# The first two output tiles of feed-forwards and mixers worked on together, and one residual taken a tile ahead

## What is computed

```python
def rmsnorm(x, g, eps=NORM_EPS):
    y = xf * lax.rsqrt(jnp.mean(xf * xf, axis=-1, keepdims=True) + eps)
    return y.astype(x.dtype) * g
def swiglu(h, w_gate, w_up, w_down):
    return (jax.nn.silu(h @ w_gate) * (h @ w_up)) @ w_down
for l in range(DEPTH):                                  # DEPTH = 2
    x = x + 0.5 * swiglu(rmsnorm(x, ffn1_norm[l]), ...)  # D_FF = 2752
    h = rmsnorm(x, mix_norm[l])
    p_a, p_b, p_c = _split(h @ w_in[l], (A_IN, B_IN, C_IN))
    ...                                                  # three mixers
    x = x + jnp.concatenate([o_a, o_b, o_c], axis=-1) @ w_out[l]
    x = x + 0.5 * swiglu(rmsnorm(x, ffn2_norm[l]), ...)
return rmsnorm(x, final_norm)
```

## Time and profile before

| | |
|---|---|
| Median of 3 runs | 4101.9 us (4096.93 to 4108.23) |
| The profiled execution | 4107.6 us |
| its span | 4105.8 us, mean granted TensorE clock 0.976 |
| TensorE busy | 3915.6 us, 95% |
| VectorE busy | 2526.2 us, 62% |
| ScalarE busy | 1961.6 us, 48% |
| GpSimd busy | 238.7 us, 6% |

### The profile page before, as it was taken

How to read it: one execution, slowest core, us unless ns; L and a number is a source line. 1 busy time by engine, 2 the same in 40 slices (tenths; PEclk the granted TensorE clock), 3 DMA queues, 4 the chain that set the end, 5 groups by cost and what they waited for, 6 DMA issues and landing times.

```text
span 4105.8 us, 60273 instructions
## 1 busy us (share of the span) xinstructions
PE 3915.6 (95%) x25080; PEld 3089.6 (75%) x25080; DVE 2526.2 (62%) x4301; ACT 1961.6 (48%) x3260; POOL 238.7 (6%) x213
## 2 busy tenths in 40 slices
PE   7999999999989999989999989999999999799998
PEld 5855778886867788868877667788788877577886
DVE  4277589995275899954456855544544469655445
ACT  3256478884364788842334434322323344343222
POOL 0033100000021000010000000000000000000000
PEclk9989999999999999999999999999999999899999
DMA  5455199992200999932222101222222221012221
GB/s 233 181 188 224 62 427 425 416 369 98 100 23 12 418 426 414 385 133 89 96 87 93 42 24 46 98 85 95 93 103 103 87 93 47 3 42 101 85 103 67
DMA packets 64297, 637.85 MB, mean 155 GB/s; under 512 B 6759, under 2 KB 7015, under 8 KB 29720
## 3 DMA queue, kind: packets, MB, share of 16 engines
q1 hardware_dynamic: 48760, 578.42, 35.9%
q0 software_dynamic: 8640, 31.46, 2.0%
q10 hardware_dynamic: 6624, 24.12, 1.4%
HBM read 603.52 MB, written 35.69 MB: 156 GB/s over the span
## 4 chain that ended last, share of the span: by engine, by line
PE 80%; DVE 12%; ACT 5%; issue 2%; DMA 2%; POOL 0%; SPq 0%; DVEq 0%; POOLq 0%; ACTq 0%
PE ps L365 13%; PE ps L370 13%; PE ps L369 13%; PE ps L1521 4%; PE ps L1523 4%; PE ps L1522 4%; DVE wbuf_r L346 2%; PE ps L1543 2%; PE ps L1542 2%; PE ps L1541 2%; PE ps L596 1%; DVE arena L3280 1%; DVE arena L3278 1%; PE ps L1054 1%; PE ps L1036 1%
## 5 line engine op out<-in xcount | busy, mean ns | idle before, releaser
L369 PE MATMUL ps<-arena_r,wbuf_r 128*128 128x512 f32 x2784 | 1089.5, 391 | 0.0
L346 DVE TENSOR_TENSOR wbuf_r<-slot,wbuf_r 128x512 fp32r<-128x512 f32 (+2 forms) x824 | 587.5, 722 | 664.6 <-ACT wbuf_r L336 663.0
L365 PE MATMUL ps<-hT_r,wbuf_r 128*128 128x512 f32 x2112 | 839.8, 398 | 19.0 <-DVE arena_r L486 13.2
L370 PE MATMUL ps<-hT_r,wbuf_r 128*128 128x512 f32 x2112 | 828.0, 392 | 0.0
L336 ACT ACTIVATE wbuf_r<-slot 128x512 fp32r<-128x512 f32 (+2 forms) x824 | 500.7, 614 | 633.9 <-PE ps L370 552.0
L369 PEld LDWEIGHTS ps<-arena_r,wbuf_r 128*128 128x128 f32 x2784 | 526.6, 189 | 109.0 <-issue 2.6
L365 PEld LDWEIGHTS ps<-hT_r,wbuf_r 128*128 128x128 f32 x2112 | 399.8, 189 | 122.1 <-DVE arena_r L486 20.9
L370 PEld LDWEIGHTS ps<-hT_r,wbuf_r 128*128 128x128 f32 x2112 | 400.1, 189 | 84.5
L365 PE MATMUL ps<-arena_r,wbuf_r 128*128 128x512 f32 x704 | 277.3, 394 | 0.9 <-DVE arena_r L2730 0.9
L370 PE MATMUL ps<-arena_r,wbuf_r 128*128 128x512 f32 x672 | 261.4, 389 | 0.0
L1387 DVE TENSOR_TENSOR wbuf_r<-arena,wbuf_r 128x1024 fp32r<-128x1024 f32 x164 | 195.4, 1217 | 58.7 <-ACT wbuf_r L1380 58.5
(11 more groups left out here) (573 smaller groups left out, 6860.2 us busy)
## 6 DMA issues: line engine op xcount, KB each, us to landing
arena<-in_moe SPq DMA_DIRECT2D x82, 2048.0 KB, 11.6
slot<-in_moe SPq DMA_DIRECT2D x52, 2048.0 KB, 11.4
slot<-in_gu SPq DMA_DIRECT2D x40, 2048.0 KB, 7.8
slot<-in_ada SPq DMA_DIRECT2D x20, 2048.0 KB, 8.3
slot<-in_down SPq DMA_DIRECT2D x16, 2048.0 KB, 7.8
...
```

The source lines that it names most:

```text
L346: v.tensor_tensor(lo[:, 0:w], src[:, off:off + w], hi[:, 0:w].bitcast(F32), ALU.subtract) \
L365: p.matmul(bank, hi[:, cs], rh[:, k, :], start=k == 0, stop=False, skip_group_check=True)
L369: p.matmul(bank, hi[:, cs], rl[:, k, :], start=False, stop=False, skip_group_check=True)
L370: t = p.matmul(bank, lo[:, cs], rh[:, k, :], start=False, stop=k == kt - 1, skip_group_check=True)
```

## The change

`two3_pe` works on the first two output tiles together. It goes through k in steps of `by` and does each step for both tiles: `by` is 4 in five stages and 1 in ffn00. To match, pieces 1 and 2 of a stage are swapped in the cutting order (tile 0's first half, tile 1's first half, tile 0's second, tile 1's second). The column sums stand behind tile 1 instead of tile 0 and the row sum behind tile 2 instead of tile 1, on all engines; in the feed-forwards three tiles are then taken out of PSUM together. In the second MoE VectorE takes the residual of dt before the remainder of dt - 2.

```diff
@@ class Cuts
-            def __init__(self, name, jobs):
+            def __init__(self, name, jobs, two=False):
                 self.name, self.jobs = name, jobs
                 self.pieces = [(j, off, w) for j, job in enumerate(jobs) for off, w in job[2]]
+                if two:
+                    self.pieces[1:3] = self.pieces[2:0:-1]
@@ new
+        def two3_pe(p, c, ps, pieces, name, tiles, rh, rl, end, by, ready):
+            bank = [ps.take((*name, i), end(i)) for i in tiles]
+            n = [[next(pieces) for _ in tiles] for _ in range(2)]
+            for j, i in enumerate(tiles):
+                for e in ps.before((*name, i)):
+                    pe.wait_ge(*e)
+            for at in range(0, 8, by):
+                for j, i in enumerate(tiles):
+                    piece = n[at // 4][j]
+                    hi, lo = pairs.buf((c.name, piece))
+                    pe.wait_ge(*dve.at(c.name, "lo", piece))
+                    for k in range(at, at + by):
+                        pe.wait_ge(*ready(k))
+                        cs = slice(k % 4 * 128, k % 4 * 128 + 128)
+                        p.matmul(bank[j], hi[:, cs], rh[:, k, :], start=k == 0, stop=False, skip_group_check=True)
+                        p.matmul(bank[j], hi[:, cs], rl[:, k, :], start=False, stop=False, skip_group_check=True)
+                        t = p.matmul(bank[j], lo[:, cs], rh[:, k, :], start=False, stop=k == 7, skip_group_check=True)
+                    if k % 4 == 3:
+                        t.then_inc(*pe.mark(c.name, "used", piece))
+                    if k == 7:
+                        pe.also(*name, i)
@@ moe_dve
             for dt in range(8):
-                if norm is not None and dt:
-                    norm_dve(v, norm, dt - 1)
+                if norm is not None and dt > 1:
+                    norm_dve(v, norm, dt - 2)
                 onto(1, dt)
             if norm is not None:
+                norm_dve(v, norm, 6)
                 norm_dve(v, norm, 7)
@@ ffn_pe
-            lin3_pe(p, m.cuts, m.ps, pieces, (n, "gu", 0), 1, hTr, nm.lo, emptied(0), ready=normed)
+            two3_pe(p, m.cuts, m.ps, pieces, (n, "gu", 0), (0, 1), hTr, nm.lo, emptied(0), 1 if n == "ffn00" else 4, normed)
             norm_col_pe(p, nm, m.ps)
-            lin3_pe(p, m.cuts, m.ps, pieces, (n, "gu", 0), 1, hTr, nm.lo, emptied(0), first=1)
+            lin3_pe(p, m.cuts, m.ps, pieces, (n, "gu", 0), 1, hTr, nm.lo, emptied(0), first=2)
             norm_row_pe(p, nm, m.ps)
@@ ffn_act (ffn_dve alike, with norm_col_dve and the wait for the row)
-                    if part or i > 1:
+                    if part or i > 2:
                         gate_up(part, i)
-                    elif i == 0:
+                    elif i == 1:
                         norm_col_act(a, m.norm, m.ps)
-                    else:
+                    elif i == 2:
                         norm_row_act(a, m.norm, m.ps)
                         gate_up(0, 0)
                         gate_up(0, 1)
+                        gate_up(0, 2)
@@ mix_proj_pe (its ScalarE and VectorE programs: column step at s == 1, row at s == 2)
+                elif s == 0:
+                    two3_pe(p, m.cuts, m.ps, pieces, (n, "proj"), m.order[0:2], hTr, nm.lo, emptied, 4,
+                            lambda k: dve.at(nm.name, "lo", k))
+                elif s > 1:
+                    lin3_pe(p, m.cuts, m.ps, pieces, (n, "proj"), 1, hTr, nm.lo, emptied, first=i)
-                if s == 0:
+                if s == 1:
                     norm_col_pe(p, nm, m.ps)
```

More of the change, by code:

```diff
@@ L2646, in ffn_plan @@
                 jobs += [tiles_job(T["down"][((w * 2 + l) * 3 + part) * 2 + s][:, 0:kt * 512], kt) for s in range(2)]
-            m.cuts = Cuts(m.name, jobs)
+            m.cuts = Cuts(m.name, jobs, two=True)
             m.sg, m.su = [ar.f(512) for _ in range(4)], [ar.f(512) for _ in range(2)]
@@ L2661, in normed @@
                 return dve.at(nm.name, "lo", k)
-            lin3_pe(p, m.cuts, m.ps, pieces, (n, "gu", 0), 1, hTr, nm.lo, emptied(0), ready=normed)
+            two3_pe(p, m.cuts, m.ps, pieces, (n, "gu", 0), (0, 1), hTr, nm.lo, emptied(0), 1 if n == "ffn00" else 4, normed)
             norm_col_pe(p, nm, m.ps)
-            lin3_pe(p, m.cuts, m.ps, pieces, (n, "gu", 0), 1, hTr, nm.lo, emptied(0), first=1)
+            lin3_pe(p, m.cuts, m.ps, pieces, (n, "gu", 0), 1, hTr, nm.lo, emptied(0), first=2)
             norm_row_pe(p, nm, m.ps)
-            lin3_pe(p, m.cuts, m.ps, pieces, (n, "gu", 0), 14, hTr, nm.lo, emptied(0), first=2)
+            lin3_pe(p, m.cuts, m.ps, pieces, (n, "gu", 0), 13, hTr, nm.lo, emptied(0), first=3)
             for part, kt in enumerate(m.kt):
@@ L2786, in mix_plan @@
             tok = rows_job(T["win"][l * 8 + 7][:, 0:8 * 264], 264)
-            m.cuts = Cuts(m.name, [jobs[0], tok, *jobs[1:], tail])
+            m.cuts = Cuts(m.name, [jobs[0], tok, *jobs[1:], tail], two=True)
             tiles = mix_order(l)
@@ L2927, in mix_proj_pe @@
                     tok3_pe(p, m.cuts, m.ps, pieces, (n, "tok"), 264, hTr, nm.lo, lambda t4: (dve, n, "tok", t4))
-                else:
-                    lin3_pe(p, m.cuts, m.ps, pieces, (n, "proj"), 1, hTr, nm.lo, emptied, first=i,
-                            ready=(lambda k: dve.at(nm.name, "lo", k)) if s == 0 else None)
-                if s == 0:
+                elif s == 0:
[4 more added lines that the diff above has]
+                if s == 1:
                     norm_col_pe(p, nm, m.ps)
-                elif s == 1:
+                elif s == 2:
                     norm_row_pe(p, nm, m.ps)
@@ L2994, in mix_proj_act @@
                     cut_hi(a, c, i)
-                if s == 0:
+                if s == 1:
                     norm_col_act(a, m.norm, m.ps)
-                elif s == 1:
+                elif s == 2:
                     norm_row_act(a, m.norm, m.ps)
-                else:
+                if s > 1:
                     i = m.order[s - 2]
@@ L3050, in mix_proj_dve @@
                     cut_lo(v, c, i)
-                if s == 2:
+                if s == 3:
                     dve.wait_ge(*act.at(m.norm.name, "row"))
-                    scaled(m.order[0])
                 if 2 <= s <= len(m.order):
```

## The result

The changed kernel takes 4080.56 us, the median of 4 runs (4077.52 to 4083.71); the kernel before took 4100.76 us beside it (4 runs, 4096.93 to 4108.23). The ratio is 0.9947, 95% interval 0.9934 to 0.9960: 20.2 us less. In a second series the same kernel gave 0.9948 (0.9932 to 0.9963). The forecast was 4084, range 4072 to 4093.

What follows compares the result with a forecast made beforehand. TensorE, busy 95% of the span, bounds the kernel, so time comes off only where it stands still or runs slowly. 3.8 + 3.45 + 4.8 + 5.2 + 3.2 = 20.4, less 1.4 = 19; 17.5 off the median gives 4084 us, range 4072 to 4093.

Steps and rivals of the forecast that it cites:

- The starts: Six places where a feed-forward or mixer begins; TensorE waited there for the norm's remainder 15 times, 13.2 us in all.
- S: Stretch at each start from tile 0's first matmul to the row sum (new order: to tile 2); 11.9 us with nothing late.
- Part 2: ffn00, behind the second MoE, residual a tile ahead: remainders about 1.9 us apart, fourth piece of weights at 1800.4, gain 3.2 us.
- the missing hold: ffn00 if GpSimd's adds did not block VectorE's two-SBUF-input instructions: 3.6 us more gain.
- the first rival: GpSimd's adds don't hold VectorE and the clock stays up: ffn00 gains 7 to 8 us; 4078 us, chance 0.17.
- Part 3: Sums a tile later: row work hidden by tile 2, tile 4's cut just hidden in feed-forwards; 0.3 us charged per feed-forward.
- the bunching: Three feed-forward tiles wait for the row instead of two, risking a late cut at tile 4; part of 1.4 us taken off.
- The sum: Gains of 20.4 us less 1.4 give 19 on the profiled run; 17.5 taken off the median.
- The adds don't hold VectorE: Rival: GpSimd's adds leave VectorE free and the clock stays up; ffn00 gains 7 to 8 us; 4078 us, chance 0.17.
- The clock takes most of it: Rival: ordinary runs keep full clock before, and the new 1.2 us waits in ffn01 and ffn11 drop it; 4092, chance 0.15.
- It doesn't do what it says: Rival: tile 1's first piece isn't ready when tile 0's half ends, so waits only change name; 4100 us, chance 0.06.
- the cuts never recover: Rival: weight cuts stay late behind the row in the four feed-forwards, making the kernel slower; 4114 us, chance 0.04.

Runs made afterwards that it cites:

- c_sums_later: The kernel before with only the column and row sums put a tile later, tiles still one behind the other: 4094.18 us, ratio 0.9981 (0.9972 to 0.9991).
- d_sums_later: The kernel before with only the sums a tile later, profiled once more: 4096.43 us in a single run with a profile.
- writes-only kernels: The changed kernel with GpSimd writing constant tiles instead of adding squares, in ffn00's norm (4075.48 us, one run) or in ffn01's (4082.51 us, one run).

## Why the prediction was right, and where it wasn't

**The starts.** The stretches forecast were 12.3, 12.35, 13.1, 13.1 and 21.1; measured 12.25, 12.26, 13.07, 13.08 and 21.12. Their sum was put at 20.4 us and is 20.7. The wait for the remainder at k=6 is gone, and the one new wait in ffn01 and ffn11 stands where it was put, 0.73 us long (with the restart behind it about the 0.95 reckoned). A part of the agreement is the point of comparison: the 0.15 us per start that S no longer contains was not in the forecast.

**Part 2.** The mechanism held and two of its sizes were off in opposite directions. Remainders came 1.7 us apart, not 1.9: I had added an undisturbed add (1.32) and the part of the remainder behind it (0.55), where an add had only 1.12 to 1.15 left once the remainder in front of it had ended. The last two remainders, which I had let pass together in 2.3 us, took 3.03, both of them held. So the last ended at 1798.95 (1798.5 forecast), and the fourth piece came at 1800.67 (1800.4). The eleven slow matmuls stand for the twelve assumed. What the part did not see is that the alternation by k is a loss in itself: 21.1 where halves give 17.0. And it prices the missing hold at 3.6 us, the first rival at 4.4; its own terms give 2.5 with the same slow matmuls (1800.4 - 1797.9) and 4.9 at full clock (8.1 - 3.2).

**Part 3.** No wait for a cut appeared at tile 4 of any feed-forward: the bunching is covered, and the 0.3 per feed-forward was not paid (the 0.15 found behind S stands at the column sums). But the part took the sums' move for free, and it is a gain: by the stretches of c_sums_later and d_sums_later against the two executions of before 1.9 + 0.4 + 1.7 and three times 1.1 (falls counted), 7.3 us, or 6.4 with the 0.15 per start taken off, and 7.8 (3.7 to 11.5) by the ratio. Taken alone, the edit that I had priced at nothing is worth a third of the whole (the edits' gains don't add up: the residual gives 5.1 alone and 2.5 on top of the others); the total was right because S contained it without being split.

**The sum.** The step that failed is the last one, from 19 on the profiled run to 17.5 on the median. The profiled run of before was 5.7 us over the median, and I put that down to half-clock time in ffn01, ffn10 and ffn11. It lay elsewhere: profiled again, ffn01 and ffn11 fell just as before, and ffn10's fall had moved to mix1; but from mix0 to ffn01 it took 4.1 us less, from mix1 to ffn11 3.8 less, and ffn00 began 4.0 earlier. Ordinary runs of before have that half-clock time, so they gain what the profiled run gains: 20.2 measured, 19.8 to 20.7 by the stretches. The other 1.4 taken off for a fall at the new short waits and for bunching were not lost either.

**The rivals.** "The adds don't hold VectorE": its time, 4078, is nearer to the result than mine (2.6 us off against 3.4), so the time alone could not tell the two apart; its reason is refuted by the writes-only kernels; it would have shown ffn00 at some 17 us, with remainders of 0.75. "The clock takes most of it": refuted, ffn01 and ffn11 keep full clock over their 0.73 us waits in every execution that had them. "It doesn't do what it says" and "the cuts never recover": refuted by the 0.17 us waits for the second piece in the mixers and by the absence of any at tile 4.

**Whether the mixers pass their gain on** can't be told from single spans: from mix0 to ffn01 eight executions with the new starts average 414.4 us (410.7 to 418.5), four with the old 415.9 (411.4 to 418.6), two of these with a fall of 1.6 at the start. From mix1 to ffn11 the same eight average 421.8 (420.1 to 423.5), the four old ones 424.3 (421.8 to 428.2). The differences, 1.5 and 2.5, have the size of the gain, 1.9, inside a spread of 8. That most of it arrives is likely, not shown; the total can't say it either, since its interval is 16 to 27 us.
